# Output projection, its norm and the network as one stage: three network pieces beside the last norm group

## The reference

```python
mix = jnp.concatenate([o_gla, o_lru, o_mla], axis=-1) @ w_out
x = _layer_norm(DEEPNORM_ALPHA * x + gate1 * mix, ln1_g, ln1_b)

h2 = x * (1 + scale2) + shift2
g_ff, u_ff = jnp.split(h2 @ ffn_w_gu, 2, axis=-1)
f = (jax.nn.silu(g_ff) * u_ff) @ ffn_w_down
x = _layer_norm(DEEPNORM_ALPHA * x + gate2 * f, ln2_g, ln2_b)
```

## Time and profile before

| | us |
|---|---|
| median of 3 runs | 3737.56 |
| lowest to highest | 3737.01 to 3742.13 |
| the profiled execution, own time | 3736.0 |
| its span | 3734.2 |
| TensorE busy (matmul), share of the span | 3409.4, 91% |
| DVE busy | 1472.0, 39% |
| ACT busy | 1161.9, 31% |
| mean granted TensorE clock | 0.95 |

### The profile page before, as it was taken

The page is one execution under the profiler, slowest core; times in us unless marked ns, Lnnn a source line. Parts: engine busy times, 40 slices in busy tenths (PEclk is TensorE's granted clock), DMA queues, the critical chain, the costliest instruction groups (busy, mean ns, idle before and its releaser), DMA issues. The chain is left out here.

```text
span 3734.2 us, 54766 instructions
## 1 busy us (share of the span) xinstructions
PE 3409.4 (91%) x22788; PEld 2936.2 (79%) x22788; DVE 1472.0 (39%) x2860; ACT 1161.9 (31%) x2170; POOL 195.5 (5%) x252
## 2 busy tenths in 40 slices
PE   2998698999979999999979869999987999999997
PEld 1885466666979999999968645666677999999997
DVE  3224665444442322232341366644445222222324
ACT  3225455443331111111231455534424211111123
POOL 0000211110000000000000111111100000000000
PEclk8998799999989999999989979989988999999998
DMA  4117100542101111111111530044310111111111
GB/s 160 48 58 249 31 1 23 192 160 78 46 29 44 47 46 40 46 42 50 34 44 34 186 122 1 1 149 168 136 46 18 40 42 50 40 46 42 49 52 49
DMA packets 79027, 255.71 MB, mean 68 GB/s; under 512 B 11275, under 2 KB 28845, under 8 KB 67894
## 3 DMA queue, kind: packets, MB, share of 16 engines
q1 hardware_dynamic: 66198, 164.04, 13.4%
q0 software_dynamic: 11520, 83.89, 6.3%
q10 hardware_dynamic: 1056, 4.19, 0.3%
HBM read 245.59 MB, written 6.51 MB: 68 GB/s over the span
## 5 line engine op out<-in xcount | busy, mean ns | idle before, releaser
L500 PE MATMUL psum<-h_hi,w_ffn_hi 128*128 128x384 f32 (+1 forms) x2112 | 697.9, 330 | 33.0 <-DVE w_ffn_lo L2320 33.0
L502 PE MATMUL psum<-h_hi,w_ffn_lo 128*128 128x384 f32 (+1 forms) x2112 | 695.0, 329 | 0.0
L501 PE MATMUL psum<-h_lo,w_ffn_hi 128*128 128x384 f32 (+1 forms) x2112 | 685.1, 324 | 0.0
L500 PEld LDWEIGHTS psum<-h_hi,w_ffn_hi 128*128 128x128 f32 x2112 | 397.9, 188 | 33.3 <-DVE w_ffn_lo L2320 33.3
L501 PEld LDWEIGHTS psum<-h_lo,w_ffn_hi 128*128 128x128 f32 x2112 | 397.9, 188 | 0.0
L502 PEld LDWEIGHTS psum<-h_hi,w_ffn_lo 128*128 128x128 f32 x2112 | 396.8, 188 | 0.0
L500 PE MATMUL psum<-ffn_act_hi,w_ffn_hi 128*128 128x384 f32 (+1 forms) x906 | 295.9, 327 | 0.0
L502 PE MATMUL psum<-ffn_act_hi,w_ffn_lo 128*128 128x384 f32 (+1 forms) x906 | 295.7, 326 | 0.0
L501 PE MATMUL psum<-ffn_act_lo,w_ffn_hi 128*128 128x384 f32 (+1 forms) x906 | 295.4, 326 | 0.0
L2335 DVE TENSOR_TENSOR ffn_act<-silu_tmp,psum 128x384 f32<-128x384 f32 x132 | 70.3, 532 | 563.2 <-PE psum L502 563.2
L486 DVE SCALAR_TENSOR_TENSOR xT<-psum,adaT,xT 128x384 f32<-128x384 f32 (+1 forms) x240 | 136.3, 573 | 391.8 <-PE psum L502 391.7
(11 more groups left out here) (391 smaller groups left out, 5949.2 us busy)
## 6 DMA issues: line engine op xcount, KB each, us to landing
w_ada_pair<-in_w_ada SPq DMA_DIRECT2D x48, 1024.0 KB, 5.0
w_ffn<-in_w_gu SPq DMA_DIRECT2D x88, 512.0 KB, 3.5
w_ffn<-in_w_down SPq DMA_DIRECT2D x32, 384.0 KB, 3.1
w_out<-in_w_out SPq DMA_DIRECT2D x16, 512.0 KB, 6.5
w_ffn<-in_w_down SPq DMA_DIRECT2D x22, 320.0 KB, 3.0
w_in_T<-in_w_in_T SPq DMA_DIRECT2D x12, 512.0 KB, 4.3
z<-in_x_prompt SPq DMA_DIRECT2D x1, 4096.0 KB
w_ada_first<-in_w_ada SPq DMA_DIRECT2D x2, 2048.0 KB, 17.2
```

The costliest lines, as they stand in the source:

```text
L500: pe.matmul(o, wh, xh, start=first, stop=False)
L501: pe.matmul(o, wh, xl, start=False, stop=False)
L502: return pe.matmul(o, wl, xh, start=False, stop=last)
```

## The change

The two stages become one, `stage_out_ffn`, with no barrier between them. Its parts:

- **Order on PE.** After the last matmul group of the output projection, the network's pieces 0 (gate 0), 1 (up 0) and 2 (gate 1) run for the token groups 0 and 1 first (six groups of matmuls, numbered g = 0 to 5, in the banks 0 to 3), then for token group 2 (g = 6 to 8), and from piece 3 on (g = 9) as before. The eight norm steps of token group 2 are put behind g = 0 to 4 (`LN1_LAST`).
- **Rounding of h by token group.** In place of eight casts and eight subtractions over 1088 columns after the norm there are 24 of each: eight of 384 columns for token group 0 (`h_rounded(0)`, `h_rest(0)`, ahead of the norm steps of group 1), eight for group 1 behind the last output group, and eight of 320 behind the norm of group 2. New semaphores `s_md` count the modulations that they wait for.
- **Weights.** The first three network pieces load into the room of `w_out` rows that are done with. For this `w_out` is stored as [output slice, k, 128] instead of [k, 1024] (each 4 KB row of a transfer is written as eight runs of 512 B), and the output slices of token group 2 come in the order 0, 5, 6, 1, 2, 7, 4, 3. SP issues network piece i (0 to 2) when output group 17 + 2i (counted from 0) is done. ACT and DVE split them beside the output groups 19, 21 and 23. Piece 3's load is issued after g = 6.
- **PSUM.** Token group 2's block 8 takes banks 4 and 5 and so waits for block 6 to be normed (`beside`), and back-turned slices 4 to 7 wait for slices 0 to 3 to be kept.

```diff
+        LAST_ORDER = (0, 5, 6, 1, 2, 7, 4, 3)
+        LN1_LAST = {0: (0, 1), 1: (2,), 2: (3,), 3: (4, 5), 4: (6, 7)}
...
+            og = [(c, n) for n in range(2) for c in range(KD)] + [(c, 2) for c in LAST_ORDER]
...
+            gg = [(i, n) for i in range(NSW) for n in range(2)] + [(i, 2) for i in range(NSW)]
+            NE = 2 * NSW
+            gg += [(i, n) for i in range(NSW, NPC) for n in pieces[i][4]]
...
+                    for k in range(KD):
+                        sp.dma_start(WOR[:, :, k, :], of("w_out")[:, k].rearrange("p (c n) -> p c n", n=P)
+                                     ).then_inc(s_ow[k], 16)
                     for i, (kind, c, f0, nk, _) in enumerate(pieces[:NLD]):
-                        if i >= IL + 4:
+                        if i < NSW:
+                            sp.wait_ge(s_om, 2 * KD + 2 * i + 2)
+                        elif i >= IL + 4:
                             sp.wait_ge(s_mm, ends[IL - 1])
...
+                    for g in range(KD, len(og)):
+                        n, at_ = divmod(g, KD)
+                        pe.wait_ge(s_ev, g - KD + 1 if g < KD + 4 else g - 3)
+                        for k in range(KD):
+                            ins = part(g, k)
+                        ins.then_inc(s_om, 1)
+                        for step in LN_BESIDE[n][at_]:
+                            ln1_pe(pe, n - 1, step)
+
                     for g, (i, n) in enumerate(gg):
...
-                        if g >= 8:
+                        if free[g] is not None:
                             pe.wait_ge(*free[g])
+                        elif g < 4:
+                            pe.wait_ge(s_ev, 2 * KD + 4 + g + 1)
+                        else:
+                            ln1_kept(pe)
                         if n == 0:
                             pe.wait_ge(s_wl, i + 1)
                         for k in range(nk):
-                            if g == 0:
-                                pe.wait_ge(s_hl, k + 1)
+                            if i == 0:
+                                pe.wait_ge(s_hl, KD * n + k + 1)
...
+                        for step in LN1_LAST.get(g, ()):
+                            ln1_pe(pe, 2, step)
...
+                        for step in LN1_LAST.get(g, ()):
+                            ln1(2, step)
+                        if g == max(LN1_LAST):
+                            h_parts(2)
+                        if NE < g < NE + NSW:
+                            split(g - NE + 2)
+                        if n == 0 and i >= NSW and i + 2 < NLD:
                             split(i + 2)
...
+                    def h_rounded(n):
+                        t0, w = GROUPS[n]
+                        act.wait_ge(s_md[0], 4 * (n + 1))
+                        act.wait_ge(s_md[1], 4 * (n + 1) + (n == 2))
+                        for k in range(KD):
+                            act.copy(HH[:, k, t0:t0 + w].bitcast(F32R), HT[:, k, t0:t0 + w]).then_inc(s_hh, 1)
...
+                    for g in range(KD, len(og)):
+                        n, at_ = divmod(g, KD)
+                        if g == 2 * KD:
+                            h_rounded(0)
+                        for step in LN_BESIDE[n][at_]:
+                            ln1_act(act, n - 1, step)
+                        if n == 2 and at_ in (3, 5, 7):
+                            split((at_ - 3) // 2)
+                    h_rounded(1)
+                    order(split, group, lambda n, step: ln1_act(act, n, step), h_rounded,
+                          lambda n, step: ln_act(act, n, step))
...
+                    for g, (c, n) in enumerate(og):
+                        at_ = g % KD
+                        dve.wait_ge(s_om, g + 1)
+                        residual(dve, lk, s_ev, TMPR, out_home(g), c, n, M_G1)
+                        if g == 2 * KD:
+                            h_rest(0)
+                        for step in LN_BESIDE[n][at_] if n else ():
+                            ln1_dve(dve, lk, n - 1, step)
+                        if n == 2 and at_ in (3, 5, 7):
+                            split((at_ - 3) // 2)
+                    h_rest(1)
...
             run(stage_mla_sample)
-            run(stage_out)
-            run(stage_ffn)
+            run(stage_out_ffn)
```

More of the change, by code:

```diff
@@ L336, in build, with group_norm @@
                      ((0, 1), (2,), (3,), (4,), (5,), (6,), (7,), ()))
-        def group_norm(name, zr, g_col, b_col, sh, sc, added):
+        def group_norm(name, zr, g_col, b_col, sh, sc, added, beside=False, md=None):
             nz = zr.shape[1]
@@ L346, in rows_psum @@
             def rows_psum(blk):
-                return bank((4, 6, 4, 4, 6, 4, 4, 6, 0)[blk], 2)
+                return bank((4, 6, 4, 4, 6, 4, 4, 6, 4 if beside else 0)[blk], 2)
             def back_psum(g, c):
-                return bank((4 + c) % 8 if g == 2 else 4 + c % 4)
+                return bank((4 + c) % 8 if g == 2 and not beside else 4 + c % 4)
             def turn(pe, blk):
@@ L358, in turn @@
                         pe.wait_ge(ed, 4 * g)
-                if blk in (2, 5):
+                if blk in (2, 5) or beside and blk == 8:
                     pe.wait_ge(nm, blk - 1)
@@ L368, in back @@
                     pe.wait_ge(nm, 3 * g + 3)
-                if c >= 4 and g < 2:
+                if c >= 4 and (g < 2 or beside):
                     pe.wait_ge(xt[c % 2], 4 * g + (c - 4) // 2 + 1)
@@ L458, in samples, with last_kept @@
                 dve.wait_ge(pm, 1)
-                dve.tensor_tensor(hs, hs, bc(ADA[:, sh:sh + KD, 1:9], ST), ALU.add)
-            return on_pe, on_act, on_dve, params, samples
+                ins = dve.tensor_tensor(hs, hs, bc(ADA[:, sh:sh + KD, 1:9], ST), ALU.add)
+                if md is not None:
+                    ins.then_inc(md[1], 1)
+            def last_kept(eng):
+                eng.wait_ge(ea, 12)
+                eng.wait_ge(ed, 12)
+            return on_pe, on_act, on_dve, params, samples, last_kept
         def modulate_prompt(eng, c, sh, sc):
@@ L2193, in stage_ffn, with out_home, out_added @@
             NPC, NLD = len(pieces), IL + KD
-            gg = [(i, n) for i in range(NPC) for n in pieces[i][4]]
-            ends = [sum(len(p[4]) for p in pieces[:i + 1]) for i in range(NPC)]
+            gg = [(i, n) for i in range(NSW) for n in range(2)] + [(i, 2) for i in range(NSW)]
+            NE = 2 * NSW
+            gg += [(i, n) for i in range(NSW, NPC) for n in pieces[i][4]]
+            ends = [max(g for g, u in enumerate(gg) if u[0] == i) + 1 for i in range(NPC)]
             GL = ends[IL - 1]
+            def out_home(g):
+                return bank(g % 8 if g < KD else g % 4)
+            def out_added(eng, n):
+                eng.wait_ge(s_ev, KD * (n + 1))
             def weights(i):
@@ L2274, in _, with order @@
                         ln_pe(pe, 2, step)
-                def order(split, group, ln):
-                    split(0)
-                    split(1)
+                def order(split, group, ln1, h_parts, ln):
                     for g, (i, n) in enumerate(gg):
                         group(g, i, n)
-                        if n == 0 and i + 2 < NLD:
+                        for step in LN1_LAST.get(g, ()):
[5 more added lines that the diff above has]
+                        if n == 0 and i >= NSW and i + 2 < NLD:
                             split(i + 2)
@@ L2320, in split, with h_rest @@
                         dve.tensor_tensor(wl.bitcast(F32R), raw, wh, ALU.subtract).then_inc(s_wl, 1)
+                    def h_rest(n):
+                        t0, w = GROUPS[n]
+                        if n == 2:
+                            ln1_samples(dve)
+                        for k in range(KD):
+                            dve.wait_ge(s_hh, KD * n + k + 1)
+                            dve.tensor_tensor(HL[:, k, t0:t0 + w].bitcast(F32R), HT[:, k, t0:t0 + w],
+                                              HH[:, k, t0:t0 + w], ALU.subtract).then_inc(s_hl, 1)
                     def rest(f, f0, n):
```

181 lines of the change are left out of this document (75 added, 106 removed).

## The result

| | before | after |
|---|---|---|
| median of the runs | 3737.28 us (3731.38 to 3742.13, 4 runs) | 3702.93 us (3699.96 to 3707.86, 4 runs) |
| time after / time before | | 0.991, 95% interval 0.9891 to 0.9929 |
| profiled execution, its own time | 3736.0 us | 3699.96 us |
| its span | 3734.2 us | 3698.2 us |

The changed kernel is faster, by 34.35 us (0.9%) between the medians, where 50.2 us were forecast. The time, 3702.93 us, lies above the forecast of 3687.4 us and outside the range of 3681 to 3697 us.

What follows compares the result with a forecast made beforehand. TensorE, busy for 91% of the span, was taken to bound the kernel, so only its idle and slow time could be won. A gain of 58.9 us less costs of 7.7 and 1.0 took 3737.56 to 3687.4 us; range 3681 to 3697.

Steps and rivals of the forecast that it cites:

- The interval, 42.15 us: From the last output matmul to the silu of piece 2 for token group 2: 42.15 us, against 72.26 and 70.91.
- the back turns, "four pairs, each 0.57 us": Token group 2's back turns between network groups: 2.28 us in all, against 7.38 at half clock.
- The waits, 0.95 us: PE's waits among the network groups: 0.35 us at block 8's turn and 0.6 at token group 2's h.
- Output group 16, 7.7 us over both: Eight subtractions ahead of the norm statistics delay block 5's turn: PE idles 3.8 us more per layer, 7.7 in all.
- rival 1: The new idle at output group 17 also drops the clock: 3 to 6 us more, 3690.4 to 3693.4 us; chance 0.22.
- w_out, 1.0 us over both: w_out loads in runs of 512 B: only the first piece is felt, 0.5 us per layer, 1.0 in all.
- Weight loads and splits of pieces 0 to 2, piece 3: Early network weight loads and splits stay hidden; piece 3 costs zero with nothing to spare, 1.1 us late at worst.
- Table loads: Four more on ACT per layer at 1.28 us each, nothing late; at 2.66 us the total gain is 2.4 smaller.
- Removed: one barrier, already counted: One barrier and one semaphore clearing fewer per layer, both inside the interval already counted, so no further gain.
- Rival 3: Clock stays at 1.2 GHz from output group 17 to piece 3: slower than before, about 3800 us; chance 0.03.
- Rival 4: A wait holds the network's first group until the norm is done: about 3714 us; chance 0.04.
- Rival 2: ACT and DVE come late among the network groups, by 1.1 or 1.2 us per layer: 3689.6 to 3692; chance 0.09.

Runs made afterwards that it cites:

- tiles: Changed kernel with token group 2's 64-row back turns put behind those of the 128-row blocks, four slices at a time; 3700.24 us, ratio 0.9883.
- later: Changed kernel with token group 0's rounding and subtraction of h moved from output group 16 to behind the norm steps of group 18; 3690.57 us, ratio 0.9864.
- half: Changed kernel with four of token group 0's eight casts and subtractions moved behind output group 18, four left ahead of the statistics; 3696.57 us, ratio 0.9876.
- runs512: Kernel before the change with only w_out laid out as in the changed kernel, in runs of 512 B; 3745.00 us, ratio 1.0012.
- before_again: Kernel before the change, unedited, profiled and timed once more; 3740.14 us, ratio 1.0001.
- again: Changed kernel, unedited, run with more executions against the kernel before; 3705.14 us, ratio 0.9906.

## Why the prediction was wrong in size and right in kind

The direction and the mechanism were right: PE is given network work at once, and the interval falls by 28.20 and 26.96 us where 30.11 and 28.76 were worked out. Point by point:

- *The interval, 42.15 us.* Measured 44.06 and 43.95. The first network matmul comes 0.15 us after the last output matmul, as the sum had it. **The step that failed here is the back turns, "four pairs, each 0.57 us".** The row it used has turns of whole blocks; group 2 has block 8 with 64 rows in each, and they took 2.22 us for twelve, 4.44 in a layer instead of 2.28. `tiles` shows the cause: ordered by size the same turns take 1.36 us. The prediction also read the 7.38 us of the earlier trace rows wrongly, as "each pair waiting for banks": that row of 24 turns has no wait inside it, only the weight loads held for 0.33 us at block 8's turns, and half of 7.38, 3.69 us, would have been nearer than 2.28.
- *The waits, 0.95 us.* At block 8's turn 0.17 us at most (the last network matmul before it starts at 1067.36 and the turn at 1067.71, 0.35 later where such matmuls follow each other in 0.17 to 0.18; 0.17 is also what a change to the 64-row tile costs elsewhere, so it may be no wait at all), and 0.20 at h of group 2: 0.6 less than forecast in each layer. Piece 3 made no wait, as said. With the back turns this gives +1.6 a layer, of the +1.9 measured in layer 0.
- *Output group 16, 7.7 us over both.* The idle is 3.76 us in each layer, against 3.84 worked out. **The failed step is that its price ended there: rival 1 came true.** The clock fell within those 3.76 us, and the matmuls at 1.2 GHz up to 1036 cost 2.7 us in layer 0 (7.0 in all, less 3.76 and the 0.5 of w_out) and 2.4 in layer 1. Rival 1 had 2.9 and 1.5. `later`, which only moves this work so that the idle goes, won 6.4 us a layer and the clock with it.
- *Why the chance was too low.* The argument for it was that the longer idle of 5.51 us still had a full clock for some 4 us, and that 1.43 us of idle within 12 had left it alone. It took the longest time for which the clock had held as the time that it would hold again. Worked out from the clock means of short stretches, it fell about 4.8 us behind the start of the idle in layer 0 of before (1054.08) and 5.2 in layer 1, but 2.8 us behind it in layer 0 of after (1026.32 to about 1029.1). `half` shows that even less was enough: 1.89 us of idle, with the fall 0.8 us after PE had started again. How long PE has idled does not by itself tell when the clock falls.
- *w_out, 1.0 us over both.* PE's wait for `w_out_lo` rose by 0.9 us in all (16.9 to 17.8), and by 0.8 in `runs512` (17.7), where the part up to the last output matmul grew by 0.5 us a layer at most. Right.
- *Weight loads and splits of pieces 0 to 2, piece 3.* No wait of PE in after names them. Right.
- *Table loads.* The timeline of ACT in after shows them at 1.28 us, the next instruction 1.30 us behind their start:

```profile
1061.23 1.28 ACT L2308 ACT_TABLE_LOAD   x1
1062.53 0.49 ACT L2308 ACTIVATE silu_tmp<-psum 128x384 f32<-128x384 f32 x1
...
1068.97 0.49 ACT L2308 ACTIVATE silu_tmp<-psum 128x384 f32<-128x384 f32 x1
1069.48 1.28 ACT L396 ACT_TABLE_LOAD   x1
1070.77 0.29 ACT L396 ACTIVATE ln_std<-mean_var,eps 64x1 f32<-64x1 f32 x1
```

  The Trainium skill, page "ScalarE: Activation LUTs", section "What ACT_TABLE_LOAD costs", gives about 2.66 us with the drain. The trace does not agree: from the end of one instruction to the start of the next it is 1.3 us (1069.46 to 1070.77), between two that wait for nothing else.
- *"Removed: one barrier, already counted."* Right for the interval, but the merged stage's end is dearer by some 0.3 us. From DVE's last modulation to the first cast of the next stage it is 4.21 us before (1905.57 to 1909.78) and 4.49 in `before_again`, 4.59 in after (1884.86 to 1889.45) and 4.74 in `again`. At the end of layer 1, up to the store of the output, it is 4.23 and 4.22 against 4.54 and 4.54 us. That is 0.6 of the 1.2 us. That more semaphores are to be cleared in the one larger stage was not tried by itself.
- *Rival 3, a clock that does not come back,* did not happen: 1.00 from 1036 to the end of the interval. *Rival 4* neither: the first network matmul follows at once. *Rival 2* neither: no wait at piece 3, and at most 0.4 us at block 8's turn and h of group 2, less than the sum had for them.

**The balance.** 50.2 us forecast less 36.0 in the profiled executions leave 14.2: 5.0 for the clock after the idle (with the small differences of the other terms there), 4.3 for the back turns less 1.2 for shorter waits and 0.6 left unassigned, 1.2 behind the silu, and 4.3 in unchanged stages. The last is chance as far as ten profiles can tell: the unchanged stages have the same mean, 1777.8 us, with the old and the new end of the layer, and the same kernel moves by more than 4.3 us between executions. What makes these stages vary was not looked for. The miss does not rest on it: with the 39.7 us of the stretches the time would have been 3697.9 us, still above the range. The range failed for a reason of its own: it took the bounds of the terms but not this scatter, which spreads single profiles over 16 us, and it treated rival 1 as an alternative, where rival 1's price (up to 3693.4) and the back turns (4.3) together already reach 3697.7.

## What to carry to other kernels

When work is put in front of a wait that has no slack, its price is the idle it makes on PE plus the restart at half clock, so look for a later place before accepting it: here the same eight subtractions two output groups later cost nothing measurable (115.07 us up to the last output matmul, where `runs512`, without them, has 114.91 and 115.14). Cost turns and small matmuls from rows of the same tile sizes in the same order, since a row of whole blocks did not hold for a mix of 128 and 64 rows. And judge an edit of a few microseconds by a stretch between fixed marks, which here repeated to 0.2 us in the changed kernel and 1.2 in the one before and in `tiles`, where the clock came back at different times, while whole executions of either differed by more than ten.

## What the runs showed of the hardware that was not expected

- The clock fell 0.8 us behind an idle of 1.89 us in `half`, when PE was at work again (0.52 in the three microseconds from 1028), and within 3.76 us in after, about 2.8 us from the start of the idle, while an idle of 1.43 us in 12 left it at 1.00 and one of 5.51 us kept it full for 4.8 us in layer 0 of before and 5.2 in layer 1. Idle length alone does not order these cases.
- The price of the half clock differs for the same idle: behind 3.76 us of idle PE was back at 2.4 GHz 5.9 us after it started again in after and in layer 0 of `tiles`, and 2.8 us after in layer 1 of `tiles`, which made 1.3 us of time.
- A weight load of 64 rows behind one of 128 rows was held 0.17 us every time at full clock and 0.33 us at half clock; twelve turns took 2.22 us alternating and 1.36 us sorted.
- The eight DMA issues of w_out take SP 4.21 us with long runs and 11.42 us with runs of 512 B; in the same layout, after has 11.52 us. Only the first piece was felt, with PE's first wait 9.1 instead of 8.6 us in `runs512`.
